# New slot numbers for the gate, S5 and GLU work inside the token-projection loop

## What is computed

```python
h = rmsnorm(x, norm_pre_mix)
proj = h @ w_in                      # columns shared out among all head groups
u, z, xbc, dt_raw, qk, v, i_raw, f_raw, o_raw = split(proj)
y_a = s5_mixer(u, ...)               # complex diagonal scan, gelu, then g * sigmoid(g @ w_glu + b_glu)
y_b = ssd_mixer(z, xbc, dt_raw, ...) # softplus(dt), cumulative sums of dt * a, chunked products
y_c = mlstm_mixer(qk, v, i_raw, f_raw, o_raw, ...)  # log-sigmoid of f, cumulative sum, running maximum
x = x + rmsnorm(concat(y_a, y_b, y_c) @ w_out, norm_post_mix)
x = x + rmsnorm((silu(n(x) @ w_gate) * (n(x) @ w_up)) @ w_down, norm_post_ffn)
```

## Time and profile before

| what | value |
| --- | --- |
| median of 3 runs | 3018.91 us (3017.41 to 3019.01) |
| the profiled execution's own time | 3019.01 us |
| its span in the profile | 3017.1 us |
| TensorE busy | 2876.0 us, 95% of the span |
| VectorE busy | 1915.8 us, 63% |
| ScalarE busy | 1196.3 us, 40% |
| GpSimd busy | 385.3 us, 13% |

### The profile page before, as it was taken

One profiled execution on the slowest core, in us unless ns is written; L12 is line 12 of the kernel. 1 busy time (PEld: TensorE's weight loads), 2 busy tenths in 40 slices (PEclk: granted clock), 3 DMA queues, 4 the chain that ended last, 5 costly groups with the idle time before them and its releaser, 6 DMA issues. The chain is left out here.

```text
span 3017.1 us, 36075 instructions
## 1 busy us (share of the span) xinstructions
PE 2876.0 (95%) x13608; PEld 2313.5 (77%) x13608; DVE 1915.8 (63%) x2608; ACT 1196.3 (40%) x2005; POOL 385.3 (13%) x496
## 2 busy tenths in 40 slices
PE   8999999999999889999699689999999999999998
PEld 4888887777777667777588568888888888888887
DVE  4777877667842467886234376666776666556756
ACT  5322222453532545453233353333433333544543
POOL 0000000013521146563012100000000000000000
PEclk9999999999999999999799889999999999999999
DMA  4222433446756667875678554444453222766863
GB/s 151 67 69 87 130 129 110 142 144 210 225 183 197 218 202 258 283 261 190 246 255 328 182 226 158 161 161 161 171 192 119 101 105 105 274 232 196 298 192 109
DMA packets 295577, 545.14 MB, mean 181 GB/s; under 512 B 59340, under 2 KB 150892, under 8 KB 286828
## 3 DMA queue, kind: packets, MB, share of 16 engines
q1 hardware_dynamic: 263644, 437.69, 43.1%
q0 software_dynamic: 24704, 75.52, 6.8%
q10 hardware_dynamic: 7056, 29.63, 2.5%
HBM read 358.30 MB, written 184.44 MB: 180 GB/s over the span
## 5 line engine op out<-in xcount | busy, mean ns | idle before, releaser
L2640 PE MATMUL f_banks<-f_bop,f_w_op 128*128 128x512 f32 x3696 | 840.2, 390 | 32.3 <-DVE f_w_op L2467 29.9
L2640 PEld LDWEIGHTS f_banks<-f_bop,f_w_op 128*128 128x128 f32 x3696 | 694.6, 188 | 177.9 <-DVE f_w_op L2467 30.3
L2648 PE MATMUL f_banks<-f_d_op 128*128 128x512 f32 x1848 | 419.0, 389 | 0.0
L2648 PEld LDWEIGHTS f_banks<-f_d_op 128*128 128x128 f32 x1848 | 346.8, 188 | 72.0
L2531 DVE TENSOR_TENSOR f_d_op<-f_d_raw,f_d_op 128x1024 fp32r<-128x1024 f32 x154 | 187.5, 1225 | 148.9 <-ACT f_d_op L2384 148.1
L1815 PE MATMUL t_banks<-t_w_hi,h_hi 128*128 128x512 f32 (+1 forms) x640 | 248.7, 389 | 10.2 <-DVE t_w_lo L1676 10.0
L656 PE MATMUL t_banks<-h_hi,c_w_hi 128*128 128x512 f32 x640 | 255.8, 400 | 0.0
L656 PE MATMUL t_banks<-h_hi,c_w_lo 128*128 128x512 f32 x640 | 250.0, 391 | 0.0
L656 PE MATMUL t_banks<-h_lo,c_w_hi 128*128 128x512 f32 x640 | 249.1, 389 | 0.0
L2384 ACT ACTIVATE f_d_op<-f_d_raw 128x1024 fp32r<-128x1024 f32 x154 | 162.9, 1061 | 198.3 <-PE f_banks L2648 161.5
L1815 PE MATMUL t_banks<-t_w_lo,h_hi 128*128 128x512 f32 (+1 forms) x640 | 238.2, 372 | 0.0
(11 more groups left out here) (351 smaller groups left out, 4579.4 us busy)
## 6 DMA issues: line engine op xcount, KB each, us to landing
f_raw<-in_w_gu SPq DMA_DIRECT2D x88, 512.0 KB, 6.4
sop<-f_a SPq DMA_DIRECT2D x154, 256.0 KB, 2.0
f_d_raw<-sop SPq DMA_DIRECT2D x154, 256.0 KB, 2.8
t_raw<-in_w_tok SPq DMA_DIRECT2D x72, 512.0 KB, 4.5
f_d_raw<-top SPq DMA_DIRECT2D x88, 256.0 KB, 3.7
m_bc<-rows SPq DMA_DIRECT2D x16, 1152.0 KB, 6.8
f_d_raw<-in_w_dn SPq DMA_DIRECT2D x66, 256.0 KB, 3.0
o_y_hi<-y_hi SPq DMA_DIRECT2D x16, 1024.0 KB, 5.0
```

Source lines behind the costliest of these rows:

```text
L2640: last = nc.tensor.matmul(bank[:, g, :], w_op[:, t % W_RING, w, cols], bop[:, s, h, k, :], start=begins and k == 0 and j == 0, stop=k == 3 ...
L2648: last = nc.tensor.matmul(banks[:, bank, :], d_op[:, d % D_RING, s, tok], d_op[:, d % D_RING, w, :], start=k == 0 and j == 0, stop=k == FU ...
```

## The change

The three pairs of slot numbers are changed. Gates begin at slot 4 instead of 6 and take 9 slots for a block instead of 11; parts A, B, C, D move to r = 0, 1, 3, 7, E to 5, the rows' stores to 6 and the transposes to 8. S5 begins at slot 44 instead of 52 with a step every third slot instead of every second, so it ends at 92 instead of 84. GLU begins at slot 99 instead of 90, with 12 slots for a block instead of 14. The loads of five small constants on SyncE move from slot 1, where they stood behind the two loads of unit 2, to the place ahead of the loop. No instruction is added or removed.

```diff
-    GATE_SLOT, GATE_STEP = 6, 11
-    S5_SLOT, S5_STEP = 52, 2
-    GLU_SLOT, GLU_STEP = 90, 14
+    GATE_SLOT, GATE_STEP = 4, 9
+    S5_SLOT, S5_STEP = 44, 3
+    GLU_SLOT, GLU_STEP = 99, 12
...
-                if 0 <= c < BLK and r == 7:
+                if 0 <= c < BLK and r == 6:
...
             c_sync(sp, ahead)
+            constants_read(sp)
+            for dst, src in ((bias[:], gate_bias), (sign[:], gate_sign), (alog[:], gate_log), (ident_sb[:], ident), (bg[:], b_glu)):
+                sp.dma_start(dst, src).then_inc(const_in, 16)
             for unit in range(UNITS):
                 for t in range(4):
                     if t < 2 and unit + 2 < UNITS:
                         load(unit + 2, t)
                     slot = 4 * unit + t
-                    if slot == 1:
-                        constants_read(sp)
-                        for dst, src in ((bias[:], gate_bias), (sign[:], gate_sign), (alog[:], gate_log), (ident_sb[:], ident), (bg[:], b_glu)):
-                            sp.dma_start(dst, src).then_inc(const_in, 16)
...
-                elif r == 6:
+                elif r == 5:
                     act.wait_ge(args_ok, c + 1)
...
-                elif r == 10:
+                elif r == 8:
                     act.wait_ge(tr_ok, c + 1)
...
-                elif r == 2:
+                elif r == 1:
                     chain(ts(u[f, :], gate_rows[IR:IR + HM, cols], bias[IR:IR + HM, :], None, add))
...
-                elif r == 4:
+                elif r == 3:
                     end, m_end = chunks(cum)[:, :, P - 1], chunks(run_max[f, :])[:, :, P - 1]
...
-                elif r == 8:
+                elif r == 7:
                     dve.wait_ge(factors_ok, c + 1)
...
-                if not 0 <= c < BLK or r != 10:
+                if not 0 <= c < BLK or r != 8:
                     return
```

## The result

The kernel after takes 3035.93 us (median of 4 runs, 3032.67 to 3036.72) against 3018.96 us for the one before: a ratio of 1.0054, 95% interval 1.0037 to 1.0073. It is 17 us slower, where 7 were forecast. The profiled execution took 3033.49 us, 2.4 us less than the median, with a span of 3031.7 us; so the profile holds 14.6 of the 17 us. From the start of the first to the start of the last matmul of the token projection (line 1815 before, 1814 after) it is 548.24 us instead of 533.86, so 14.4 of the 14.6 us by which the spans differ lie in the stage that was changed.

A forecast was written before the change was run, and what follows sets the result against it. TensorE, busy 95% of the span, was taken as the bound, so its waits decide. Gates +20.2, S5 -2.0 and GLU -11.2 summed to +7.0 us on 3019.0: 3026 us, own range 3020 to 3032, whole range 3012 to 3038.

The forecast's parts named there:

- first rival: Slots 118 to 128: step 8's `g`, the `w_out` parts and the mask collide again, no relief; 3037 us, chance 0.13.
- three signs of being wrong: No wait at slot 8; transposes waiting under 10 us in all; `t_w_lo` waits staying near slots 120 to 128.
- Gates: Gate blocks cut from eleven slots to nine: the part loses 29 us where it lost 8.8, +20.2 us.
- The walk: Tally of the gate chain, slots 4 to 39: block waits of 8.6, 5.6, 7.2 and 4.2 us, 25.6 in all.
- all falls of the clock: Gate blocks: half clock after gaps, some 2.4 us a fall, expected at the 6.3 and 7.2 us gaps; 3.4 us taken.
- S5 and the first operands: Waits for the first S5 operands (1.5 us) and before the first GLU step (0.5 us) go: -2.0 us.
- The zero for the step: S5 step every third slot instead of every second: saves TensorE nothing, taken as 0.
- GLU: GLU from slot 99, twelve apart: of 12.2 us lost at the late GLU steps 1 stays, -11.2 us.
- The end of the stage: GLU steps end at slot 141, not 138; last `y` stored about with the last tile: 0, up to 1 us.
- the gates cost less: Rival: the gate chain waits less on ScalarE, stage loses 20 to 24 us; about 3019 us, no change; chance 0.20.
- faster: Rival: the chain fits into nine slots, gates cost 8.8 us as before; 3006 us, chance 0.12.
- the mask would meet VectorE again: Slot 124: the mask meets step 8's product or unit 32's weights; some 5 us over after a hold of 6.

The follow-up runs named there:

- e1: Kernel after with S5 and GLU back at 52, 2 and 90, 14, leaving the gates' new places and early constants; 3039.63 us, ratio 1.0067.
- e4: Kernel after with S5 every second slot from slot 60, instead of every third from 44; 3039.34 us, ratio 1.0069.
- e2: Kernel before with only GLU moved, to slot 99 with 12 slots a block; 3013.96 us, ratio 0.9984.
- e7: Kernel before with GLU at 99, 12 and the mixers' first loads from slot 108 instead of 112; 3005.25 us, ratio 0.9959.
- e10: Kernel after with the mixers' first loads from slot 108 instead of 112; 3026.42 us, ratio 1.0033.
- e8: e7's kernel with gate blocks of 12 slots instead of 11 and S5 from slot 57 instead of 52; 3018.35 us, ratio 0.9994.
- e9: e8's kernel with S5 from slot 56 instead of 57; 3003.37 us, ratio 0.9955.

## Why the prediction was right, and where its sum was off

**How right.** The forecast was 3026 us, its own range 3020 to 3032, the whole range 3012 to 3038. The measured 3035.93 is outside the forecast's own range and nearer to the first rival's 3037, which had a chance of 0.13. It is inside the whole range because that was drawn to take in this rival. None of the three signs of being wrong came (the wait at slot 8 is there, the transposes wait 12.3 us, no weights are late near slots 120 to 128). But I had written that line 1874 would wait for nothing, and it waited 4.8 us.

**Gates: right in the places, 2 us too low, and in part by two errors that cancel.** The walk had 6.3 us at slot 8; it was 6.06. At unit 5's weights it had 2.7, measured 2.70; at block 2's transposes 7.2, measured 7.45; at block 3's 3.7, measured 3.27; slot 40 was to begin near 696 us and began at 697.1 in an execution whose stage started 1.0 us later. Only the transposes of blocks 0 and 1 waited less, 0.7 and 0.9 for 2.1 and 2.9: there a fall of the clock had used up the time first, as the walk said that it might. The term as a whole was +20.2; by the stretches it is 31.0 - 8.8 = +22.2, and e1's stage, 21.8 us longer with the GLU waits of before, agrees. Two errors stand against each other in it: the walk's waits were 25.6 us and 21.9 came, and I took 3.4 us for all falls of the clock where they cost some 9. The price of one fall, 2.4 us, was about right. The count was not: I gave a fall to the gaps of 6.3 and 7.2 us alone, but around the gaps of 2.7 and 3.3 us the clock fell too (0.80 from 620.0 to 628.4 us, 0.59 from 693.5 to 701.9). In e1's stage the 1.5 us for the first S5 operands are gone as well.

**S5 and the first operands: right.** -2.0 predicted. Neither wait is in the profile after. The zero for the step holds for S5's old place; e4 shows 3.4 us at another.

**GLU: the mechanism right, its size off; this is the term that was off most.** The 12.2 us at slots 118 to 129 did go. But I let 1 us of it stay, and slot 123 took 12.56 us for 5.80: 6.8 us, 4.84 of wait and the rest half clock. So the term was -5.4, not -11.2; e2's stage, 6.3 us shorter with the first `g` wait of 0.5 us gone and 4.0 us at step 8, agrees. I had reckoned `g` to be wanted 17 us after the fourth step and gave its reload no time in the queue. What I left out stands in the prediction's own order of issues: the stores of `y` and the operands of the chunk are ahead of the reload on the same queue, and with the constants at 112 all of them were issued late; that a store's late landing would hold VectorE, and through it SyncE, is not in the prediction at all. e7 and e10 take that queue's load away and the wait with it. It is half of my first rival ("step 8's `g` ... collide again"), at half its price.

**The end of the stage: 0 held.** Behind the last matmul of the stage the span is 1931.9 us after and 1932.7 before.

**The sum.** +22.2 - 2.0 - 5.4 = +14.8, measured in the stage +14.4. The medians differ by 17.0, with an interval of the ratio of 11 to 22 us; the 2.6 us that the profile doesn't hold are not explained. The rivals "the gates cost less" and "faster" are out: e1. That the mask would meet VectorE again, with time over, was right: step 8's product took 6.15 us in the kernel after, and TensorE didn't wait for it.

## What to carry to other kernels

Work that is put into slots by hand is a chain over several engines: add up its operations, round trips and what stands ahead of each on its engine, and give it as many slots as the whole takes, since an engine busy 22 of 32 us can still be the one that is waited for. Count the small waits too: here gaps of 2.7 and 3.3 us came with half clock as the long ones did. A slot number also says which other work it is queued behind, and one slot to the side was worth 18 us of the stage here, 12 of the whole by the ratios (e8 and e9). And a load has to be judged by what its queue holds at that moment, and by what the loads ahead of it wait for, not by its distance to the use.

## What the runs showed of the hardware

One VectorE operation was held for the whole of a run of GpSimd operations, as in the earlier trace rows: in the kernel after the GLU product of line 1774 took 6.15 us beside six mask operations of GpSimd that took 5.84, where the same operation otherwise takes 1.2. It began after them (1021.69 against 1021.03), where the one of the earlier trace rows began before (1014.24 against 1014.64), so by these two rows it doesn't depend on who begins:

```profile
1021.69 6.15 DVE L1774 TENSOR_TENSOR t_arena<-t_arena 128x512 f32<-128x512 f32 x1 [1.12 <-ACT t_arena L1638]
```

```profile
1021.03 5.84 POOL L1030 TENSOR_TENSOR m_bc<-m_bc,m_mask 128x384 f32<-128x384 f32 x6
```

The issue of a DMA on SyncE's queue is not a fixed cost: the stores of `y` took 0.4 to 0.5 us each at free places, and in the kernel after 3.8 and 4.7 us while the DMA engines were full (a share of 0.92 and 1.07 over these two issues). Full engines alone are not enough for it: other issues between 983 and 994 us took 0.4 to 0.6 us. What makes the difference is open.

The clock fell around TensorE's long gaps and not at once. In the kernel after TensorE stood from 654.6 to 662.0 us; the granted clock was still 1.00 from 655.5 to 656.5, then 0.52 from 656.5 to 667.0 us, and 0.98 in the 3 us behind it, so about 5 us of work behind the gap ran at half clock.
